# Splitting streamed weight units three units ahead of TensorE instead of two

## The reference

```
h = rms_norm(x, g_mix);  proj = h @ w_in                     # q, k, v, z, f, scal, gates
y_a = gated_deltanet_branch(...);  y_f = fourier_branch(...)  # ... @ w_dn_up, ... @ w_fourier
x = x + (gate_a * y_a + gate_f * y_f) @ w_o
x = x + square(relu(rms_norm(x) @ w_mlp_up)) @ w_mlp_down
x = rms_norm(x, g_final)
# second block
proj = rms_norm(x) @ w_in_2                                   # a_u a_v a_g b_x b_g x_q x_g gates
y_a = spatial gating;  y_b = s5 state space;  y_x = attention over a memory of 256 rows
merged = sum(sigmoid(gate_n) * (y_n @ w_branch_n))            # n = 0, 1, 2
x = x + rms_norm(merged @ w_out)
```

## Time and profile before

| | us |
|---|---|
| median of three runs | 2645.27 |
| the profiled execution | 2644.37 |
| its span, first to last instruction | 2642.6 |
| TensorE busy in it | 2550.9 |
| VectorE busy | 1649.5 |
| ScalarE busy | 1059.2 |

### The profile page before, as it was taken

How to read it: one execution, slowest core, us unless ns; L and a number is a source line. 1 busy time by engine, 2 the same in 40 slices (tenths; PEclk the granted TensorE clock), 3 DMA queues, 4 the chain that set the end, 5 groups by cost and what they waited for, 6 DMA issues and landing times.

```text
span 2642.6 us, 29766 instructions
## 1 busy us (share of the span) xinstructions
PE 2550.9 (97%) x12186; PEld 2115.6 (80%) x12186; DVE 1649.5 (62%) x1640; ACT 1059.2 (40%) x895; POOL 368.2 (14%) x372
## 2 busy tenths in 40 slices
PE   7989999899999999999999999999999999999998
PEld 6768887688778788888888888888888788888776
DVE  5385566854667755445544557689999964445564
ACT  4543325433234353443344344443332445544332
POOL 0002310131000000000000000027878500000000
PEclk9999999999999999999999999999999999999999
DMA  6332225332465445555555555666555566566553
GB/s 244 124 115 101 102 101 176 111 104 88 140 240 215 185 175 191 191 190 190 187 186 188 191 187 200 217 240 210 180 187 182 188 253 243 176 244 233 199 223 143
DMA packets 84645, 478.63 MB, mean 181 GB/s; under 512 B 8752, under 2 KB 8880, under 8 KB 32944
## 3 DMA queue, kind: packets, MB, share of 16 engines
q1 hardware_dynamic: 84528, 476.99, 50.2%
HBM read 453.88 MB, written 23.07 MB: 180 GB/s over the span
## 4 chain that ended last, share of the span: by engine, by line
PE 74%; DVE 16%; DMA 4%; issue 4%; ACT 2%; SPq 0%; DVEq 0%; ACTq 0%
PE acc L1974 21%; PE acc L1976 21%; PE acc L1975 21%; DVE w_lo L1237 4%; PE banks L2154 4%; DMA raw<-in_w 3%; PE banks L2177 2%; DVE prod L1754 2%; ACT w_hi L792 2%; PE banks L1985 1%; DVE squares L1453 1%; DVE convT L1443 1%; DVE prod L1748 1%; PE banks L2085 1%; DVE prod L1747 1%
## 5 line engine op out<-in xcount | busy, mean ns | idle before, releaser
L1237 DVE TENSOR_TENSOR w_lo<-raw,w_hi 128x2048 fp32r<-128x2048 f32 x396 | 915.1, 2314 | 643.6 <-ACT w_hi L792 642.6
L792 ACT ACTIVATE w_hi<-raw 128x2048 fp32r<-128x2048 f32 x396 | 755.2, 1913 | 632.7 <-DMA raw<-in_w 632.5
L1974 PE MATMUL acc<-w_hi,a_hi 128*128 128x512 f32 x2112 | 850.5, 403 | 32.4 <-DVE w_lo L1237 24.5
L1976 PE MATMUL acc<-w_hi,a_lo 128*128 128x512 f32 x2112 | 827.5, 392 | 0.0
L1975 PE MATMUL acc<-w_lo,a_hi 128*128 128x512 f32 x2112 | 827.0, 392 | 0.0
L1974 PEld LDWEIGHTS acc<-w_hi,a_hi 128*128 128x128 f32 x2112 | 400.0, 189 | 128.0 <-DVE w_lo L1237 22.2
L1976 PEld LDWEIGHTS acc<-w_hi,a_lo 128*128 128x128 f32 x2112 | 398.9, 189 | 85.9
L1975 PEld LDWEIGHTS acc<-w_lo,a_hi 128*128 128x128 f32 x2112 | 400.0, 189 | 81.0 <-issue 1.9
L1974 PE MATMUL acc<-w_hi,b_hi 128*128 128x512 f32 x928 | 365.1, 393 | 0.0
L1976 PE MATMUL acc<-w_hi,b_lo 128*128 128x512 f32 x928 | 362.4, 391 | 0.0
L1975 PE MATMUL acc<-w_lo,b_hi 128*128 128x512 f32 x928 | 362.2, 390 | 0.0
(11 more groups left out here) (329 smaller groups left out, 2026.3 us busy)
## 6 DMA issues: line engine op xcount, KB each, us to landing
raw<-in_w SPq DMA_DIRECT2D x396, 1024.0 KB, 4.8
spilled<-stage SPq DMA_DIRECT2D x72, 256.0 KB, 6.0
gate_in<-spilled SPq DMA_DIRECT2D x20, 512.0 KB, 4.1
b_pad<-in_b_pad SPq DMA_DIRECT2D x8, 512.0 KB, 5.8
x_rows<-in_x SPq DMA_DIRECT2D x4, 512.0 KB, 9.7
x_rows<-in_x SPq DMA_DIRECT2D x1, 2048.0 KB, 12.2
mem_rows<-in_mem SPq DMA_DIRECT2D x2, 1024.0 KB, 4.8
spilled<-stage_b SPq DMA_DIRECT2D x8, 256.0 KB, 6.0
```

The costliest lines, as they stand in the source:

```text
L792: act.activation(w_hi[:, n % HIGH, :], raw[:, n % RAW, :], ACT.Copy)\
L1237: dve.tensor_tensor(w_lo[:, n % RAW, :], raw[:, n % RAW, :], w_hi[:, n % HIGH, :].bitcast(F32), ALU.subtract).then_inc(lo_split, 1)
L1974: pe.matmul(o, hi[:, tk], wh, start=first, stop=False)
L1976: ins = pe.matmul(o, lo[:, tk], wh, start=False, stop=last)
```

## The change

ScalarE and VectorE split unit n+3 in slot n instead of unit n+2. The split of unit 2 moves in front of slot 0. Nothing else is different: the same instructions, buffers, semaphores and waits, in another order on two engines.

```
@@ -33,7 +33,7 @@
-AHEAD = 2
+AHEAD = 3
@@ -1069,6 +1069,7 @@          (ScalarE)
             rows_in("x", 0)
             split(0)
             split(1)
+            split(2)

             def slot_work(n):
                 run_steps(me, steps, 2 * n)
```

## The result

The changed kernel takes 2752.01 us (median of four runs, 2744.15 to 2757.3) where the kernel before takes 2645.23 on the same chip: a ratio of 1.0397, 95% interval 1.0384 to 1.0410. It is 106.8 us slower; 92 were forecast, and the range was 2690 to 2780. The profiled execution took 2757.3 us, 5 above the median, so sizes read from it are on average a little large.

The account below looks back on a forecast made before the run. The prediction took TensorE as hardly ever still, but the gate-load ring, not TensorE, as deciding in places. Its terms 38 + 35 + 5 + 8 + 6 sum to 92 us, giving 2737 us, range 2690 to 2780.

Parts of the forecast that it names:

- The ring as what pays: Stages with gate loads: a closed loop of weight load, split, emptying and gate load sets the time and gets longer.
- The turn: One round from gate load to gate load grows from 13.3 us to between 15.8 and 17.3; 15.8 taken.
- Term A: `w_branch` stage: late entry, nine longer turns, then TensorE waits for the last `y_rows`; 38 us lost.
- Term B: `w_fourier` and `w_dn_up` stage: late entry, longer turns, `x_rows` load in the last turn, 2 for `y_in`; 35 us lost.
- Term C: Units 99 to 102: the emptying of 99, for which `mlp_in` waits, stands behind the split of 102; 5 us.
- Term D: State space and gating: begins 5 us later (bounds 2.5 and 6.5), `sg_norm` behind one more split, 2.3; put at 8.
- Term E: Small ends: split of unit 2 before `x`'s second quarter, second-half convolutions, emptying before the second `hidden`; 6 us together.
- The solver: Delta-rule solver: units last 8 to 15 us, so 9.0 fit; 0 lost, bounds 0 and 2.3 for each half.
- The list of signs: Turns about 15.8 us, SyncE's waits up 40 or more, TensorE's `w_lo` idle from 24.5 to over 60, MLP loop unchanged.
- Late once: Gate-load stages: SyncE still reaches the weight load in time, turn stays 13.3, delay paid once; 2677 us, chance 0.10.
- Faster: TensorE's waits for `w_lo`, less the 6.9 us at the start, vanish: 17.6 us, giving 2627; chance 0.04.
- Longer turns: Second loads 3.95 us late as a rule, 14 turns cost 1.5 more each, TensorE's clock may drop; 2765 us, chance 0.17.

Follow-up runs that it names:

- `gates_late3`: The changed kernel with SyncE's gate loads (but the first two of each block) two slots later, behind the two weight loads they stood before; 2667.3 us.
- `empty_first3`: The changed kernel with the emptying before the slot's split on ScalarE and VectorE, three units ahead kept everywhere; 2696.3 us.
- `two_places`: The kernel before, with three units ahead only in slots 96 to 110 and 309 to 317, two everywhere else; 2662.4 us.

## Why the prediction was right, step by step

**The ring as what pays** was right in its place, its cause and its kind. It is shown by three kernels that each break or shorten it with the rest of the change in force (gates two slots later, gates one slot later, emptying first), and by the one that has the change in these slots alone.

**The sum** was short. The five stretches of the profiled execution add up to 113 us, 21 more than the terms, and the medians differ by 106.8, 15 more. Every term was exceeded or met, so the total doesn't owe its agreement to errors that cancel: the two stages with gate loads, 73 of the 92 us, were 8.6 short, and terms C and D nearly all of the rest.

**The turn** was forecast at 15.8 us, with 17.3 as the other bound. In the `w_branch` stage SyncE's pair for unit 361 was issued at 2487.12 and that for 379 at 2633.79: nine turns in 146.7 us, 16.3 each, where 142.2 were forecast. One of the nine, with the load of `post_gain` between the two weight loads, took 19.0 alone, and the other eight 15.96 on average. Letting the extras cancel was the small mistake. The price of the second load was right: ScalarE began the second of a pair 2.59 us after the first at one place of the timeline and 2.46 at the next. Of the nine pairs before the load of 379, seven are 2.43 to 2.71 us apart, one is 3.65 (in the turn of 16.56 above), and the one with `post_gain` between 5.63.

```profile
2557.59 1.91 ACT L792 ACTIVATE w_hi<-raw 128x2048 fp32r<-128x2048 f32 x1 [11.46 <-DMA raw<-in_w]
2560.18 1.91 ACT L792 ACTIVATE w_hi<-raw 128x2048 fp32r<-128x2048 f32 x1 [0.68 <-DMA raw<-in_w]
2573.36 1.92 ACT L792 ACTIVATE w_hi<-raw 128x2048 fp32r<-128x2048 f32 x1 [11.28 <-DMA raw<-in_w]
2575.82 1.91 ACT L792 ACTIVATE w_hi<-raw 128x2048 fp32r<-128x2048 f32 x1 [0.54 <-DMA raw<-in_w]
```

1.05 MB in 2.46 us are 426 GB/s. The prediction weighed this against the 358 GB/s of a page of the Trainium skill. Another page of the Trainium skill, "Perfetto Trace Analysis" (Roofline), says that one core alone may go beyond its share up to about 435 GB/s of its 16 DMA engines. By that an estimate for 1 MB is 2.4 us, and this trace agrees with that page and not with the 2.9 us of the smaller figure.

**Term A** (`w_branch`): 44.0 us measured, 38 forecast. The entry was right to a microsecond: taking off the lag of 68.9 that unit 316 had, unit 361 was issued at 2418.2, forecast 2417.4. The nine turns carry 4.5 of the 6 us of difference, the entry 0.8. The expected waits in the middle of a unit for `y_rows` before `merge_in` are there.

**Term B** (`w_fourier`, `w_dn_up`): 37.6 measured, 35 forecast. Unit 77 was issued at 740.22, less the 4.9 of lag 735.3 (forecast 735.4), unit 87 at 831.03, less 4.9 826.1 (forecast 823.6). The step of `heads_norm` that was to come 12 us late shows as TensorE's longest new wait, 15.2 us, and unit 76 is 12.3 us later for it. In `gates_late3` the lag still grows by 5.4 us by unit 76, so of the 12.3 at that unit about 7 belong to SyncE's late pair and 5 to the place behind the split of 77. The load of 2 MB for `x_rows` between two weight loads was put at 5 us; in the changed kernel's chain the weight load behind it takes 14.19, against 7.7 to 9.5 for a second of a pair in the `w_branch` stage, so it came to some 5 to 6:

```profile
808.69 0.47 SPq L613
...
809.26 0.38 SPq L616
...
809.68 14.19 DMA raw<-in_w
```

**Term C** (units 99 to 102): 5 forecast, and unit 101 is 5.2 us later for the reason given; with the emptying ahead of the split (`empty_first3`) it is 2.3 later. But the stretch to unit 112 lost 11.2, 9.0 in `two_places`, and term E had only 1.3 of it. The 3.3 us at unit 109 were missed. The chain of the changed kernel goes from VectorE's statistics of `mem_rows`, which now stand behind further splits and end at 984.3, over ScalarE to its first emptying into `hidden` at 986.21, and TensorE stands 2.5 us before the products on `hidden`. This is read from the chain; no kernel undid it alone. `empty_first3`, where the emptying stands ahead of the split on both engines, loses 0.8 us at unit 109 instead of 3.3, which fits.

**Term D** (state space and gating): 8 forecast (its two parts, 5 and 2.3, make 7.3), 15.3 measured, the step that was mis-sized most. Up to unit 314 the lag grew by 6.0 us, where 5 were forecast for the begin. But `sg_norm` was counted as "behind a split more, 2.3", that is at VectorE's price, not at the price of that split's load. Its statistics stand behind the split of unit 315, whose load SyncE issues after the loads for the gating. In the chain of the changed kernel:

```profile
2180.37 14.50 DMA raw<-in_w
...
2194.89 1.92 ACT w_hi L792
...
2196.84 2.29 DVE w_lo L1238
2199.13 2.39 DVE stats L1276 x4
```

14.5 us for a load, since 4.5 MB for `av`, `au`, `ag`, `ln_gb` and `w_sg` were issued just ahead of it. Before, the same statistics began at 2123.74, behind the split of unit 314, whose load was issued ahead of all that. The lag grew by 9.3 us over units 315 and 316 for it, and by as much in `two_places`.

**Term E** up to unit 57: 4.9 measured, 4.6 forecast, but within the scatter of that column; nothing follows from the agreement.

**The MLP loop** at 0: right, 533.3 us in both kernels. **The solver** at 0: the kernels don't contradict it, and can't show it to better than 5 us. The units of its first half (20 to 39) took 7.4 to 20.9 us before, not 8 to 15, so the 9.0 us of a late split don't fit in all of them; between units 24 and 48 the changed kernel lost nothing all the same.

**The list of signs.** SyncE's waits were to grow by some 40 us or more; they grew by 84. TensorE's idle time before `w_lo` was to rise from 24.5 to over 60; it rose to 29.5 in the page's group, and this sign was wrong. The reason was in the prediction's own ring: what is late isn't the split, it is what stands behind the split. TensorE's new idle time ends with `y_rows` (23.1 us), `heads` (15.2) and the inputs of products.

**The rivals.** "Late once" fails by the turns of 16 us. "Faster" took the 17.6 us of TensorE's waits for `w_lo` as the stake; three units ahead on ScalarE alone, in the slots before 53, does win 8.5 us, so there was something in it. With VectorE three ahead as well, the same stretch shows no gain (4.9 us lost, within the scatter). "Longer turns" lies 13 us above the measured median and the forecast 15 below, so the total doesn't choose between them; the turns do. Second loads were not 3.95 late as a rule, but in its other part this rival was right: the granted clock did fall. Busy us per stretch, units 73 to 88 and 363 to 380 of the changed kernel, and then the same units before:

```profile
721.60:857.80 136.20, 101.34 (x426) 82.31 (x425) 66.66 (x55) 37.87 (x29) 0.00 (x0) 0.86 0.47 181
2515.50:2655.30 139.80, 110.27 (x437) 87.39 (x438) 66.96 (x54) 38.84 (x28) 0.00 (x0) 0.90 0.44 173
```

```profile
716.90:815.30 98.40, 94.10 (x425) 77.05 (x424) 65.48 (x56) 35.78 (x27) 0.00 (x0) 0.98 0.66 251
2437.10:2542.30 105.20, 97.30 (x439) 79.15 (x437) 59.11 (x48) 36.88 (x26) 0.00 (x0) 1.00 0.57 224
```

The granted clock is 0.86 and 0.90 of full speed instead of 0.98 and 1.00, and nearly the same matmuls (420 to 440 recorded in each) keep TensorE busy for 7.2 and 13.0 us longer. In the ring that should be mostly idle time turned into busy time, since TensorE isn't what the turn waits for; no run tested it. Whether it has a part in the 6 us by which term A was short can't be told from these runs.

## What to carry to other kernels

To run a step earlier in an in-order list is only earlier if its input is there. Here the loads were still issued at the same moment, four buffers deep, so one unit more ahead on VectorE moved the waiting forward and everything behind it back. Before moving a step that waits, list what stands behind it on its engine, and look for a loop: here emptying, gate load, weight load, split, emptying. When such a ring is found, break it where it is cheapest (an issue that needs a late semaphore goes behind those that don't); and price each wait by the landing of that one load, with everything queued ahead of it, not by the average landing time.

## What the runs showed that was not expected

Standing as such cost nothing in the `w_branch` stage: over its whole time the kernel with late gates and three units ahead has ScalarE waiting 1024 us for loads and VectorE 821 for ScalarE, and TensorE is busy for 95.80 of 95.80 us in the stage where the changed kernel lost 44.

The same 1 MB weight load took 4.8 us at the median, mostly 5.7 to 6.4 behind a gate load, 7.7 to 9.5 as the second of a pair behind it, and 14.2 or 14.5 behind 2 MB of `x_rows` or the loads for the gating, each from issue to landing.

The same order of instructions up to unit 57 came out 4 to 5 us apart in two profiled executions, while the MLP loop was the same to 0.1 us in eleven of the twelve kernels of the table (533.2 to 533.3; 534.7 with ScalarE alone three units ahead).
